# Three attentions of a multi-layer network: from one head at a time to pairs of heads

## The reference

```python
# first block, layer 1: neighbourhood attention, 8 heads of 64
s = concat([q @ k_band + bias, q @ k_ctx])      # 512 positions with bias or mask, 256 of context
o = softmax(s) @ concat([v_band, v_ctx])
# second block, layer 0: forgetting attention, 16 heads of 64, causal
s = q @ k.T * scale + c[query] - c[key]         # c: running sum of log-sigmoid gates
h = h + (softmax(causal(s)) @ v) @ w_out
# second block, layer 1: sparse attention, 16 heads of 64, keys and values in 2 groups
o = g0 * (p_c @ v_cmp) + g1 * (softmax(causal(q @ ks.T)) @ vs) + g2 * (softmax(window(q @ kw.T)) @ vw)
h = h + o @ w_out                               # g0, g1, g2: sigmoid gates by token and head
```

## Time and profile before

| | us |
|---|---|
| median of 3 runs | 4700.32 |
| lowest, highest | 4699.89, 4703.68 |
| span of the profiled execution | 4685.8 |
| TensorE busy | 3930.5 (84%) |
| VectorE busy | 2126.0 (45%) |
| ScalarE busy | 1089.3 (23%) |
| GpSimd busy | 412.4 (9%) |

### The profile page before, as it was taken

How to read it: one execution, slowest core, us unless ns; L and a number is a source line. 1 busy time by engine, 2 the same in 40 slices (tenths; PEclk the granted TensorE clock), 3 DMA queues, 4 the chain that set the end, 5 groups by cost and what they waited for, 6 DMA issues and landing times. The chain is left out here.

```text
span 4685.8 us, 71716 instructions
## 1 busy us (share of the span) xinstructions
PE 3930.5 (84%) x30102; PEld 2911.1 (62%) x30102; DVE 2126.0 (45%) x4202; ACT 1089.3 (23%) x2092; POOL 412.4 (9%) x399
## 2 busy tenths in 40 slices
PE   5967876999977887978977777799899967798998
PEld 2855673444457774868953222488687757786877
DVE  2368953000044456656552000246476235574762
ACT  1122322000022312222210000226322123363221
POOL 0011000111102001414200000011000001000000
PEclk7988787999989997979888999999999967898999
DMA  7121017999940211000049999710232221002322
GB/s 283 37 92 28 1 59 310 384 392 395 394 141 32 73 55 59 3 6 3 2 151 392 401 401 399 295 37 1 82 95 94 70 63 39 1 2 86 95 91 80
DMA packets 203311, 658.53 MB, mean 141 GB/s; under 512 B 27220, under 2 KB 110548, under 8 KB 153320
## 3 DMA queue, kind: packets, MB, share of 16 engines
q1 hardware_dynamic: 185264, 614.97, 35.0%
q0 software_dynamic: 13056, 34.66, 2.8%
q10 hardware_dynamic: 4672, 4.33, 0.3%
HBM read 624.96 MB, written 28.41 MB: 139 GB/s over the span
## 5 line engine op out<-in xcount | busy, mean ns | idle before, releaser
L3098 DVE TENSOR_TENSOR w_lo<-ffn_landing,w_hi 128x1024 fp32r<-128x1024 f32 x132 | 161.4, 1225 | 292.6 <-ACT w_hi L3076 292.6
L3050 PE MATMUL ffn_ps<-ffn_inT_hi,w_hi 128*128 128x512 f32 x704 | 275.8, 392 | 9.2 <-DVE w_lo L3098 9.2
L3050 PE MATMUL ffn_ps<-ffn_inT_lo,w_hi 128*128 128x512 f32 x704 | 275.3, 391 | 0.0
L3050 PE MATMUL ffn_ps<-ffn_inT_hi,w_lo 128*128 128x512 f32 x704 | 275.1, 391 | 0.0
L1743 PE MATMUL up_ps<-w_quarter,rowsT 128*64 128x512 f32 x1024 | 239.7, 612 | 37.0 <-DMA w_quarter<-in_moe_w 37.0
L1743 PE MATMUL gate_ps<-w_quarter,rowsT 128*64 128x512 f32 x1024 | 236.0, 606 | 29.4 <-DMA w_quarter<-in_moe_w 20.6
L1743 PE MATMUL down_ps<-w_quarter,hiddenT 128*64 128x512 f32 x1024 | 235.0, 598 | 29.6 <-DMA w_quarter<-in_moe_w 27.6
L1353 ACT ACTIVATE prob<-score_ps,negmax 128x256 f32<-128x256 f32 (+4 forms) x272 | 166.5, 612 | 234.1 <-DVE negmax L1326 233.7
L1268 PE MATMUL probT_ps<-ident,prob 128*128 128x128 f32 x896 | 157.6, 293 | 62.7 <-ACT probT L1344 57.6
L1866 DVE TENSOR_TENSOR gain_then_hidden<-up_ps,gain_then_hidden 128x768 f32<-128x768 f32 (+1 forms) x32 | 26.4, 825 | 353.3 <-PE up_ps L1755 179.6
L1743 PEld LDWEIGHTS down_ps<-w_quarter,hiddenT 128*64 128x64 f32 x1024 | 68.6, 136 | 187.0 <-issue 129.4
(11 more groups left out here) (672 smaller groups left out, 8857.9 us busy)
## 6 DMA issues: line engine op xcount, KB each, us to landing
w_quarter<-in_moe_w SPq DMA_DIRECT2D x384, 1024.0 KB, 16.8
ffn_landing<-in_f_w_up SPq DMA_DIRECT2D x88, 512.0 KB, 3.5
ada_landing<-in_ada_w SPq DMA_DIRECT2D x24, 1024.0 KB, 12.9
ada_ring<-in_ada_w SPq DMA_DIRECT2D x24, 1024.0 KB, 5.4
ffn_landing<-in_f_w_down SPq DMA_DIRECT2D x44, 512.0 KB, 3.5
w_landing<-in_od_w_in SPq DMA_DIRECT2D x13, 1024.0 KB, 10.0
w_landing<-in_a_w_in SPq DMA_DIRECT2D x12, 1024.0 KB, 5.4
w_landing<-in_ev_w_in SPq DMA_DIRECT2D x6, 1024.0 KB, 5.5
```

Of the source, the lines that this page charges most:

```text
L3050: mm = nc.tensor.matmul(ps[c % 4][:, :], w[:, c % NP, cols], h[:, k, :], start=(k + i == 0), stop=(k == KD - 1 and i == 2))
L3098: nc.vector.tensor_tensor(wl[:, c % NP, :], land[:, c % NL, :], wh[:, c % NP, :].bitcast(F32), ALU.subtract).then_inc(split, 1)
```

## The change

A new stage `paired_attention` takes the place of `attention` for the three attentions named; the first layer's attention keeps the old one.

- Its units go by pairs of heads: (head 2k, head 2k + 1) of the same query tile. In the sparse attention a group has both branches of both heads, four units.
- The values are the stationary operand (64 columns) and the turned probabilities stream (128 columns). The two heads write to PSUM partitions 0 to 63 and 64 to 127 of one bank, in turn key tile by key tile. The result of a group is so 128 features x 128 tokens: what `turn` made. It accumulates over a whole group.
- As the result is turned, it can't be scaled by row; GpSimd multiplies the probabilities in place by the inverse sum (and the gate) before they are turned.
- Score buffers: 4 (2 for the neighbourhood attention), exponentials 2 ahead (1), probability buffers 4, turned SBUF buffers 4, two PSUM buffers for turning with 512 (384) columns each, so a neighbourhood unit's copy is in two pieces. The maximum comes negated in one instruction where there is no bias.
- VectorE copies the result of a group out, some units later (`LAG`), as a high and a low half where the projection wants them.
- The three `turn` stages go. `Early` transfers are issued at the start of the attention stage.
- `compressed_attention` ends with the copies of the turned probabilities, which now hold the gate too; its value product is the opening product of each sparse group, in the same PSUM tile.

The core of the diff (the new stage's lists of TensorE, ScalarE, GpSimd and VectorE, and its calls):

```diff
+def paired_attention(nc, groups, ident, early=None, spare=None):
+    units = [u for g in groups for u in g[1]]
...
+    NS = 4 if BANKS == 1 else 2
+    AHEAD = 2 if BANKS == 1 else 1
+    SB, ST, SM = 4, 4, 8
...
+        @block.sync
+        def _(sp):
+            if early is not None:
+                early.load_first(sp)
...
+            def scores(i):
+                if i >= NS:
+                    pe.wait_ge(probs, i - NS + 1)
+                for lhsT, rhs, a, b, start, stop in units[i][0]:
+                    mm = nc.tensor.matmul(score(i, a, b), lhsT, rhs, start=start, stop=stop, skip_group_check=True)
+                mm.then_inc(scored, 1)
+
+            def turn_probs(i):
+                pe.wait_ge(normed, i + 1)
+                for k in range(first[i], first[i + 1]):
+                    _, a, b = chunks[k]
+                    if k >= 2:
+                        pe.wait_ge(tkept, k - 1)
+                    for c in range(a, b, P):
+                        mm = nc.tensor.transpose(pt[k % 2][:, c - a:c - a + P], pr[:, i % SB, c:c + P], ident)
+                    mm.then_inc(turned, 1)
+
+            def values(c):
...
+                if fresh:
+                    if g >= 2:
+                        pe.wait_ge(done, g - 1)
+                    for lhsT, rhs in opening:
+                        nc.tensor.matmul(out[:, 0:P], lhsT, rhs, start=True, stop=False, skip_group_check=True)
+                pe.wait_ge(tkept, first[2 * c + 2])
+                steps = units[2 * c][1] // P
+                for j in range(steps):
+                    for y in range(2):
+                        i = 2 * c + y
+                        mm = nc.tensor.matmul(out[64 * y:64 * y + 64, 0:P], units[i][2][j], pT[:, i % ST, j * P:(j + 1) * P],
+                                              start=(fresh and not opening and j == 0), stop=(last and j == steps - 1),
+                                              skip_group_check=True)
+                mm.then_inc(summed, 1)
+
+            for i in range(NS):
+                scores(i)
+            for i in range(N):
+                if i + NS < N:
+                    scores(i + NS)
+                turn_probs(i)
+                if i % 2 == 0 and i:
+                    values(i // 2 - 1)
+            values(N // 2 - 1)
...
+            for i in range(AHEAD):
+                exponential(i)
+            for i in range(N):
+                if i + AHEAD < N:
+                    exponential(i + AHEAD)
+                copy(i)
...
+        @block.gpsimd
+        def _(pool):
+            for i, u in enumerate(units):
+                p = pr[:, i % SB, 0:u[1]]
+                pool.wait_ge(inv, i + 1)
+                if u[4] is None:
+                    nc.gpsimd.tensor_scalar(p, p, ri[:, i % SM:i % SM + 1], None, ALU.mult).then_inc(normed, 1)
+                else:
+                    nc.gpsimd.tensor_scalar(p, p, ri[:, i % SM:i % SM + 1], u[4], ALU.mult, ALU.mult).then_inc(normed, 1)
...
+            def maximum(i):
...
+                if bias is None:
+                    nc.vector.reduce_max(mx[:, m:m + 1], score(i, 0, n), AX_X, negate=True).then_inc(maxed, 1)
+                    return
...
+            def keep(g):
+                to = groups[g][2]
+                dve.wait_ge(summed, couples_to[g])
+                if len(to) == 1:
+                    nc.vector.tensor_copy(to[0], po[g % 2][:, 0:P]).then_inc(done, 1)
+                    return
+                nc.vector.tensor_copy(to[0], po[g % 2][:, 0:P]).then_inc(hi_kept, 1)
+                dve.wait_ge(hi_kept, g + 1)
+                nc.vector.tensor_tensor(to[1], po[g % 2][:, 0:P], to[0].bitcast(F32), ALU.subtract).then_inc(done, 1)
+
+            kept = 0
+            for i in range(N):
+                maximum(i)
+                if i:
+                    inverse(i - 1)
+                if kept < len(groups) and i >= 2 * couples_to[kept] + LAG:
+                    keep(kept)
+                    kept += 1
...
 # neighbourhood attention
-                attention(nc, units, ident, 1.0)
-                turn(nc, [([O[:, t, k * P:(k + 1) * P] for t in range(LT)], catT[:, 4 + k, :], None)
-                          for k in range(4)], ident)
+                paired_attention(nc, [([], [unit(2 * k, t), unit(2 * k + 1, t)], (catT[:, 4 + k, t * P:(t + 1) * P],))
+                                      for k in range(H8 // 2) for t in range(LT)], ident)
...
 # forgetting attention
+        spare = x[:, LT:NT, :].rearrange("p t d -> p (t d)").rearrange("p (i n) -> p i n", n=SEQ)
+        paired_attention(nc, [([], [unit(2 * k, t), unit(2 * k + 1, t)],
+                               (oh[:, k, t * P:(t + 1) * P], ol[:, k, t * P:(t + 1) * P]))
+                              for k in range(KD) for t in tiles], ident, early, spare)
         c1.close()
-        early = Early(nc, ctx, "a_out", 2, [KD // 2, 512], split_pieces(d["a_w_out"]))
-        turn(nc, [([O[:, t, k * P:(k + 1) * P] for t in tiles], (hh[:, k, :], hl[:, k, :]), None)
-                  for k in range(KD)], ident, split=True, early=early)
-        add_split(nc, hh, hl, d["a_w_out"], x, tiles, early)
+        add_split(nc, oh, ol, d["a_w_out"], x, tiles, early)
...
 # compressed_attention: the value product and gated copy out
-            for t in range(LT):
-                pe.wait_ge(tkept, t + 1)
-                if t:
-                    pe.wait_ge(kept, t)
-                for q in range(4):
-                    mm = nc.tensor.matmul(po[:, q // 2, q % 2 * 256:(q % 2 + 1) * 256], ET[:, t, q, :],
-                                          vb[:, q // 2, :], start=True, stop=True, skip_group_check=True)
-                mm.then_inc(out, 1)
...
+            rows = sm[:, :].rearrange("p (t h) -> p t h", h=H16)
+            chain(tt(rows, rows, gate, ALU.mult))
             tt(Ef, Ef, sm[:, :].unsqueeze(2).broadcast_to(wide), ALU.mult).then_inc(probs, 1)
-            for t in range(LT):
-                dve.wait_ge(out, t + 1)
-                tt(O[:, t, :].rearrange("p (h v) -> p h v", h=H16),
-                   po[:, :, :].rearrange("p a (h v) -> p (a h) v", v=64),
-                   gate[:, t, :].unsqueeze(2).broadcast_to([P, H16, 64]), ALU.mult).then_inc(kept, 1)
...
 # sparse attention
+        paired_attention(nc, [([(vb[:, k // 4, k % 2 * P:(k % 2 + 1) * P], ET[:, t, k // 2, :])],
+                               [unit(*branch, 2 * k + y, t) for branch in ((1, ksh, ksl, VS), (2, kwh, kwl, VW)) for y in range(2)],
+                               (oh[:, k, t * P:(t + 1) * P], ol[:, k, t * P:(t + 1) * P]))
+                              for k in range(KD) for t in tiles], ident, early)
+        add_split(nc, oh, ol, d["b_w_out"], x, tiles, early)
```

More of the change, by code:

```diff
@@ L26 @@
 H16 = 16
+LAG = 4
 class Stage:
@@ L2917, in _, with causal_unit @@
             nc.vector.tensor_tensor(negs[32:32 + H16, :], ab[:, :], negs[0:H16, :].bitcast(F32), ALU.subtract)
-def causal_units(qs, kh, kl, kv_of, v_of, out_of, extra, identR, causalR):
-    units = []
-    for h in range(H16):
-        g = kv_of(h)
-        for t in range(LT):
-            n = (t + 1) * P
-            q = qs[:, h, t * P:n]
-            mms = [(q, kh[:, g, 0:n], 0, n, True, False), (q, kl[:, g, 0:n], 0, n, False, False)]
-            mms += extra(h, n)
-            mms.append((identR, causalR, t * P, n, False, True))
-            units.append((mms, n, [v_of(h, i) for i in range(t + 1)], out_of(h, t)))
-    return units
+def causal_unit(qs, kh, kl, g, h, t, values, extra, gate, identR, causalR):
+    n = (t + 1) * P
+    q = qs[:, h, t * P:n]
+    mms = [(q, kh[:, g, 0:n], 0, n, True, False), (q, kl[:, g, 0:n], 0, n, False, False)]
+    mms += extra
+    mms.append((identR, causalR, t * P, n, False, True))
+    return mms, n, [values(i) for i in range(t + 1)], None, gate
 def forgetting(nc, d, x, cst, arrived):
@@ L2950, in forgetting @@
         qs = hs[:, :, :, :].rearrange("p a k t -> p (a k) t")
-        V, Q = (sb(n, [P, LT, D]) for n in ("fa_v", "fa_q"))
-        c1 = ctx.enter_context(ExitStack())
-        K = sb("fa_k", [P, LT, D], c1)
-        F = sb("fa_f", [H16, SEQ], c1)
-        negs, identR, causalR, sel = (sbr(n, [P, w], c1) for n, w in (("neg_sums", SEQ), ("ident_r", P), ("causal_r", P),
+        V = sb("fa_v", [P, LT, D])
+        with nc.sbuf_tensor("fa_out_hi", [P, KD, SEQ], F32R) as oh, nc.sbuf_tensor("fa_out_lo", [P, KD, SEQ], F32R) as ol:
+            pass
+        Q, K = (sb(n, [P, LT, D]) for n in ("fa_q", "fa_k"))
+        F = sb("fa_f", [H16, SEQ])
+        negs, identR, causalR, sel = (sbr(n, [P, w]) for n, w in (("neg_sums", SEQ), ("ident_r", P), ("causal_r", P),
                                                                   ("head_row", H16)))
@@ L3291, in compressed_attention @@
         tkept = st.sem("turned_kept")
-        out = st.sem("summed")
-        kept = st.sem("kept")
         chained = st.sem("chained")
@@ L3459, in sparse_attention @@
```

(2 more changed lines are left out.)

138 lines of the change are left out of this document (106 added, 32 removed).

## The result

| | kernel before | changed kernel |
|---|---|---|
| median, first comparison (5 and 5 runs) | 4700.32 | 4671.43 (4652.05 to 4687.37) |
| ratio, 95% interval | | 0.9943 [0.9915, 0.997] |
| median, second comparison (11 and 6 runs) | 4700.31 | 4663.97 (4656.03 to 4672.68) |
| ratio, 95% interval | | 0.9919 [0.9902, 0.9936] |
| span of the profiled execution | 4685.8 | 4662.4 |

The changed kernel is faster by 29 to 36 us, where 82 were forecast; 4671 lies at the upper end of the range, 4590 to 4672. The forecast's sum can be taken apart in the two profiled executions. In the table a stage runs from the start of its first score to the start of its last value pass; the sum of the last column is the change of the span.

A forecast was written before the change was run, and what follows sets the result against it. TensorE was taken to set the pace; terms of -21.6, -12.1, -20.2, -3.0, -16.7, -13.0 and +4.5 us sum to -82.1, giving a span of 4603.7 and a median of 4618 us; 8-in-10 range 4590 to 4672.

The forecast's parts named there:

- the multiplication lies beside it at both ends, and only the order could expose it: Paired attentions: GpSimd's multiply stays hidden beside TensorE's work but for starts and ends, +4.5 us in three stages.
- the waits: Neighbourhood attention: 7 of 10 us of TensorE waiting go, 4 come back for the longer road through VectorE and GpSimd.
- GpSimd's price: GpSimd's multiply of the probabilities: bounds 0.84 and 2.2 ns a column from its copy and tensor product, 1.5 taken.
- rival A: Attentions: the chain exponential, VectorE, GpSimd, transpose becomes the bound; half of 54 us kept, 4645 us; chance 0.18.
- Values: Value passes of the three attentions: 0.055 us each with overlapping halves, saving 21.5, 17.9 and 35.8 us.
- Changes of form: TensorE's switches between 128x64 and 128x128, two per pair of heads: 0.09 us each, +2.9, +5.8 and +11.5 us.
- Sparse attention with the seam: Sparse attention -20.2 us, and its two branches becoming one stage -3.0 us.
- Turns and compressed attention: Turn stages removed: 6.6, 6.6 and 3.5 us go; value products and gated copies leaving the compressed attention: 13.0 us.
- The span and the median: Whole kernel: the timed median lies 14.5 us above the profiled span, so a span of 4603.7 gives 4618 us.
- C: Attentions: GpSimd's multiply at 4.4 ns a column sets the pace, +32 us, 4732 us; chance 0.07.
- B: Value passes: column halves don't overlap at 128 columns, all of the 75 us return, 4693 us; chance 0.08.
- My own mark for being wrong: The four attentions together: the forecast is wrong if they shrink by under 35 us or over 75.

The follow-up runs named there:

- e1: Changed kernel with GpSimd's gateless multiply given a second operation, times 1.0: 4639.45 us, ratio 0.9864; neighbourhood stretch 99.9 us.
- e2: Changed kernel with the neighbourhood attention's transposes one unit later on TensorE and ScalarE's exponential one unit further ahead: 4631.94 us, ratio 0.9849.
- e3: Changed kernel with the edits of e1 and e2 together: 4605.78 us, ratio 0.9816; neighbourhood stretch 76.4 us.
- e5: On top of e3, value passes issued one column half after the other in all three paired attentions: 4644.77 us, ratio 0.9876.
- the two edits: On the changed kernel, the second operation in GpSimd's gateless multiply (e1) and the later neighbourhood transposes with earlier exponential (e2): 4605.78 and 4615.40 us.
- e9: The kernel of e3 run again, beside the changed kernel on the same chip: 4615.40 us, ratio 0.9808.

## Why the prediction was wrong

The forecast is wrong by 53 us (46 by the second comparison), and nearly all of it is one step: "the multiplication lies beside it at both ends, and only the order could expose it", with the waits priced at +4. I compared GpSimd's load with TensorE's and took the look-ahead in units. What counts with two score buffers is the length of the ring through all engines, 4.98 us and the multiply, against TensorE's 4.38 for two units. Even at my 1.5 ns a column (1.4 us) it would have been 6.4, no better than the 6.26 of before. The ring could have been added up beforehand from the earlier trace rows: transposes, values, scores, maximum with bias, and the inverse in the queue behind it.

- **GpSimd's price.** Bounds 0.84 to 2.2 ns a column; measured 2.5 for one operation and 0.84 for two (603 ns at 128 columns and 2203 at 768 for one, 372 and 904 for two in e1). The copy's and the tensor product's rows did not bound the form. Cost by e1: some 37 us of the neighbourhood stretch (19 of ring, the rest clock) and 6 of the forgetting attention, whose -7.3 instead of -12.1 this explains. But e2 shows the price is not the cause by itself: with a longer look-ahead it is nearly hidden. The lock on a shared port pair that stands beside rival A shows in no row: the 32 multiplies of 768 columns last 2188 to 2205 ns, whatever VectorE does beside them.
- **The clock.** No step had it. The waits cost 16 us more than their own length.
- **Values.** 0.055 us a pass, as forecast; answering to the earlier trace rows:

```profile
L1455 PE MATMUL out_ps<-probT,fa_v x320: 272/273/324, 3228.3 to 3313.3; 128*64 128x128 f32 x160
L1455 PE MATMUL out_ps<-probT,v_win x320: 272/273/324, 4057.7 to 4206.8; 128*64 128x128 f32 x160
```

- **Changes of form.** Forecast 0.09 us each. In e3 the last transpose starts at 1533.36 + 0.82 - 0.27 = 1533.91 and the first value pass 0.20 later, where 0.11 is the pace: 0.09. From the last value pass to the scores it is 0.20 as well (1562.36 + 1.26 to 1563.82 in the changed kernel). The rule of the Trainium skill that spoke against the change (TensorEngine Tiling (Array Packing), Key Properties) is right in kind, and its price is this.
- **Sparse attention with the seam.** -21.7 forecast (with its start), -24.0 measured. Here the gate gave GpSimd the fast form and four score buffers the look-ahead.
- **Turns and compressed attention.** -6.6 and -13.0 forecast; -6.6 and -13.1 measured at the rows above. The whole stretch from the forgetting to the sparse attention is 16.5 shorter and not 19.6; where the other 3 us are I have not traced.
- **The span and the median.** I read 14.5 us as time outside the span. It is 2 us (4664.45 against 4662.4 in the changed kernel's profiled execution); the rest was that the profiled execution of before was a quick one among spans of 4681.9 to 4712.8. As the median of before less the 82.1 gives 4618 as well, this misreading doesn't touch the forecast's difference.
- **Slack.** VectorE has 19% of the time free in the sparse attention, less than the quarter I gave as the least. It did no harm there.
- **Rivals.** A named the mechanism, the place and the two score buffers, but priced it at 27 us over the forecast (4645). Half of 54 us was a share, not a sum over a ring. C put the point where the kernel becomes slower at 4.0 ns a column; the neighbourhood attention by itself crosses it where 4.98 us and the multiply reach 6.26, which by e1's fixed 0.27 us is 1.3 ns a column. B is refuted by e5. My own mark for being wrong (the four attentions shrink by under 35 us) was met: three went from 381.8 to 383.7 us, the compressed one lost 13, together 11. That 4671 is still inside the range by 1 us is luck: the width was set by other prices than the ones that came.

With the two edits the kernel comes near the forecast: 4605.78 and 4615.40 us, against 4618. It isn't the forecast's sum in each term: the neighbourhood attention shrinks by 27 to 28 us where 20 were forecast, because all of its 10 us of waits go, where I let 3 go on balance.

## What to carry to other kernels

When a step is put between two engines, add up the whole ring from its output back to its next input, over every queue it passes and in the order of each queue, and divide by the number of units that are in flight; engines that are each under 80% busy say nothing. If buffers can't be added, issue the waiting instruction one place later. Measure a new instruction's exact form, its number of operations included, before trusting a neighbouring one, and look at the granted clock where TensorE waits: here the waits cost 16 us more than their own length.

## What the hardware showed that I had not expected

- GpSimd's tensor-scalar on float32: one operation 603 ns at 128 columns and 2203 at 768 (2.5 ns a column), by a per-partition factor or by a constant (1491 at 512); two operations 372 and 904 with a constant as the second factor, 449 and 770 (at 512) with two per-partition factors (0.83 to 0.84 ns a column). The Trainium skill (GPSIMD Engine Reference, Performance versus the Vector engine) gives about 1.03 cycles an element for the shortest bodies and 2.6 for two inputs, 0.86 and 2.2 ns by its 1.2 GHz; the two-operation form agrees with the first, the tensor product of the earlier trace rows with the second, and the one-operation form is slower than both.
- Passes with 64 stationary columns start 0.11 us apart in one column half and 0.055 in alternation, at 128 streamed columns; where one half's passes follow the other's, some of them overlap as well (0.065, e5).
- The recurrence, unchanged in all kernels, ran at a granted clock of 0.83 to 0.85 in six profiled executions and of 0.79 to 0.80 in six, and the stretch that holds it took 1588 to 1606 or 1617 to 1623 us. The same kernel showed both (e3 and e9). What selects it stays open.
